# Nine projections of a two-layer block turned from plain fp32 products into three passes over high and low parts

## The chip, the cores and the metric

The kernel runs on one core of a Trainium2 chip. The metric is the device time of one execution in microseconds (us). TensorE multiplies matrices into PSUM (eight banks of 128 x 512 fp32), ScalarE and VectorE work element by element and read PSUM, GpSimd works element by element on SBUF and issues some of the transfers, SyncE issues the stream of weights.

## The reference

Two transformer models of two layers each, one after the other, on 256 tokens of width 1024, all in fp32. Every mixer and every feed-forward is preceded by an RMS norm with a shift and a scale made from a conditioning vector, and followed by a gated residual:

- layer 1: gated linear attention (`gla`), then PEER (`peer_q0`, `u0`, `v0`: product-key routing over 16384 one-neuron experts);
- layer 2: sliding-window attention (`kv`, `swa_q`, `swa_out`), then PEER (`peer_q1`, `u1`, `v1`), then the last norm of the first model;
- layer 3: an mLSTM mixer (`ml_qk`, `ml_v`, `ml_o`, `ml_out`), then a squared-ReLU MLP (`ffn1_0`, `ffn2_0`);
- layer 4: latent attention (`qa` to `ukv_v`, `mla_out`), then an MLP (`ffn1_1`, `ffn2_1`).

A name in brackets is a weight matrix. Those that matter here:

```
gla_out, swa_q, swa_out, ml_v, ml_o, ml_out, mla_out:  y[256,1024] = h[256,1024] @ W[1024,1024]
kv:      y[256,512]  = h[256,1024] @ W[1024,512]
ml_qk:   y[1024,256] = W[1024,1024].T @ h.T   (kept transposed)
```

## The kernel before, in words

All weights stand in one stream in HBM, in slabs of 128 x 2048 fp32 (1 MB), in the order of `PLAN`. SyncE loads them in two halves of 512 KB into `ring`, which has room for two slabs. A half is called a tile (128 x 1024). TensorE is used in two ways:

**Plain.** `gemm_M` and `gemm_T` (lines 580 and 602) multiply the fp32 slab in `ring` as it is. TensorE reads `ring` itself, and SyncE may refill a slab when TensorE has used all of it (`slab_used`).

**In three passes.** The names in `SPLIT` (the PEER and MLP matrices). For each tile ScalarE writes `split_hi` (the tile rounded to fp32r, line 1258), and VectorE or GpSimd writes `split_lo` = tile - `split_hi` (line 1283 on VectorE, in `v0`, `v1` and the second half of `u0`, `u1`; line 1271 on GpSimd, elsewhere). The activations have such parts too. TensorE then adds hi x hi, hi x lo and lo x hi, each product one fp32r matmul. There are two buffers each of `split_hi` and `split_lo`; the semaphores `hi_made`, `lo_made`, `hi_free`, `lo_free` count tiles, and SyncE may refill a half of `ring` when its `split_lo` is made.

The order of work on every engine is written out by hand, and each engine runs its own list in order. Beside the mixers VectorE adds up the conditioning strips ("side chunks", line 426, transfers of 512 KB issued by GpSimd, line 412, into four slots): 16 in the `swa` stage, 40 in `ml`, 24 in `mla`. An out-projection (`*_out`) goes as follows: TensorE turns the mixer's output into PSUM, VectorE copies it to `yT` (line 550), TensorE and VectorE spread the gate over the partitions (lines 453, 464, 472), TensorE multiplies with `last_by_tile=True` (the last products in an order that ends one output bank after the other), VectorE gates and adds the residual bank by bank (lines 692, 703, 705), and the next norm follows. In `peer_q` and `ffn1` the first tile waits for ScalarE's `hi` part of the activations (line 788) and for VectorE's full value and `lo` part (lines 781, 800, `parts_vector`).

```
def used_up(a, tiles, n, e):
    if tiles is None:
        return slab_used, n + (PLAIN[a])
    return lo_made, n * 2 + (tiles + e + 1)
```

Of the kernel before, what the change touches and what calls it, by code (L numbers as in the profile page):

```python
# [34 lines left out]
P = 128  # L35
# [37 lines left out]
SPLIT = ["peer_q0", "u0", "v0", "peer_q1", "u1", "v1", "ffn1_0", "ffn2_0", "ffn1_1", "ffn2_1"]  # L73
# [7 lines left out]
for _name, _n in PLAN:  # L81
    if _name in SPLIT:
# [13 lines left out]
SIDE_STRIPS = {"swa": [10, 11], "ml": [19, 20, 21, 26, 27], "mla": [23, 24, 25]}  # L96
ORDER = (list(range(FIRST_STRIPS)) + V_STRIPS[0] + SIDE_STRIPS["swa"] + V_STRIPS[1] + SIDE_STRIPS["ml"]
         + SIDE_STRIPS["mla"])
# [29 lines left out]
def build(nc, io, marks):  # L128

    new_marks = {}  # L130
    with ExitStack() as ctx:
# [8 lines left out]
        with ExitStack() as scope:  # L140
            scope.enter_context(nc.sbuf_tensor("mlp_room", [P, MLP_ROOM], F32))
            mlp_hi, mlp_lo = (scope.enter_context(nc.sbuf_tensor(n, [P, DC, SEQ], F32R)) for n in ("mlp_hi", "mlp_lo"))
            hid_hi, hid_lo = (scope.enter_context(nc.sbuf_tensor(n, [P, FF // P, SEQ], F32R)) for n in ("hid_hi", "hid_lo"))
        gate = sb("gate", [P, KEYS * SEQ])
# [68 lines left out]
        LAYER = common.at  # L213
        fin_row = yT.rearrange("p a b -> p (a b)")[:, 0:D]
# [415 lines left out]

        def half(nb):
            return slice(nb * BANK, (nb + 1) * BANK)
# [259 lines left out]
        b_flat = b_.rearrange("p a b -> p (a b)")  # L892
        NCH = SEQ // CHUNK

        def gla_tensor(t):
# [71 lines left out]
            gemm_M(t, "gla_out", "gla_out", DC, 2, D, yT, lambda c: [f"gla.on.T{c}"], bank=0, last_by_tile=True)  # L967
# [15 lines left out]
        def gla_scalar(a):  # L983
# [42 lines left out]
            std_scalar(a, "gla.r", 8)  # L1026

        def gla_vector(v):
# [54 lines left out]
            for n in range(NCH - 1):  # L1083
# [18 lines left out]
                .then_inc(vector_steps, v.step())  # L1102
            rstd_vector(v, "gla.r", DV, 8)
# [10 lines left out]
            turned_vector(v, "gla.on", yT, bank=4)  # L1114
            row_store(v, "g1_0", 0)
            v.wait_ge(vector_steps, v.n)
# [36 lines left out]
        def split_gemm_T(t, name, weights, blocks, hi, lo, nbanks=4):  # L1153


            for b in range(blocks):
# [9 lines left out]
                def passes(w, part, src, first=False, last=False):  # L1166
                    for c in range(DC):
                        t.wait_ge(*when(f"{name}.{part}{c}"))
                        ins = nc.tensor.matmul(out, w[:, b % 2, c * P:(c + 1) * P], src[:, c, :],  # L1169
                                               start=(first and c == 0), stop=(last and c == DC - 1))  # L1170
                        if c == 0 and w is split_lo and b or c == DC - 1 and last and not b:
                            ins.then_inc(hi_free, 1)
                    return ins
                passes(split_hi, "hi", hi, first=True)
# [3 lines left out]
                if b:  # L1178
                    passes(split_lo, "hi", hi, last=True).then_inc(lo_free, 1)
                else:  # L1180
                    passes(split_lo, "hi", hi)
                    passes(split_hi, "lo", lo, last=True)
                    nc.tensor.matmul(ps[:, 4, 0:P], zeros[:, :], zeros[:, :], start=True, stop=True).then_inc(lo_free, 1)
# [162 lines left out]
        def peer_choose_vector(v, l):  # L1346
# [5 lines left out]
            parts_vector(v, f"n2_{l}", hT, hT_hi, hT_lo, 4, scale_c, MOD1[l] + SH2, f"pq{l}")  # L1352
# [1312 lines left out]
```

## Time and profile before

| | |
|---|---|
| time, median of 3 runs | 2868.77 us (2868.17 to 2874.35) |
| time of the profiled execution | 2856.19 us |
| its span in the profile | 2854.6 us |
| TensorE busy | 2663.9 us (93% of the span) |
| VectorE, ScalarE, GpSimd busy | 1939.4, 1059.7, 863.3 us |
| mean granted TensorE clock | 0.964 |

The span is what the profiler sees of the program, and the profiled execution's own time is 1.6 us longer. A busy share is one of the whole span; what an edit is worth is read in its own stage. A timeline row gives the start, the duration, the engine, the line, the output and inputs, and in brackets how long the engine had been idle and what released it. TensorE's plain fp32 matmuls have two records each.

### The profile page before, as it was taken

To read this page: it belongs to the slowest core of one execution; us is meant where nothing else is said; L and a number is where in the kernel's file an instruction comes from. 1 tells how busy PE (TensorE), PEld (TensorE's weight loads), DVE (VectorE), ACT (ScalarE), POOL (GpSimd) and SP (SyncE) were. 2 spreads that over 40 slices of the span, in tenths; PEclk is the share of its full clock that TensorE was granted. 3 is DMA by queue.
4 is the path that set the end of the run, shared out by engine and by line. 5 is a ranking of instruction groups with operands and counts; after the bars stand their busy time and mean duration, and the time that the engine had idled before them with its cause. 6 is when DMAs were issued, how large, how long until landed. Compare 5 with 4: busy or idle time off the path is not lost.

```text
span 2854.6 us, 50064 instructions
## 1 busy us (share of the span) xinstructions
PE 2663.9 (93%) x17946; PEld 2258.7 (79%) x17946; DVE 1939.4 (68%) x3229; ACT 1059.7 (37%) x1549; POOL 863.3 (30%) x525
## 2 busy tenths in 40 slices
PE   5988999999999998899999999999988799988898
PEld 4458999999877874679999998778875489755886
DVE  6422997777898774536977778997773579054880
ACT  1214444433434442234444434434441144321443
POOL 2005995000000001047990000000011058810687
PEclk9989999999999998789999999999999899989999
DMA  8524555444467776154555545667876445563454
GB/s 341 214 74 148 170 178 182 160 159 164 167 217 241 273 271 220 36 171 155 177 179 167 161 155 171 207 220 256 274 249 252 175 145 180 193 232 106 148 183 148
DMA packets 147620, 536.83 MB, mean 188 GB/s; under 512 B 16784, under 2 KB 17168, under 8 KB 147232
## 3 DMA queue, kind: packets, MB, share of 16 engines
q1 hardware_dynamic: 115088, 417.08, 43.9%
q0 software_dynamic: 31104, 113.26, 11.4%
q10 hardware_dynamic: 1296, 4.72, 0.4%
q8 instruction: 84, 1.38, 0.2%
q14 instruction: 48, 0.39, 0.0%
HBM read 531.85 MB, written 3.15 MB: 187 GB/s over the span
## 4 chain that ended last, share of the span: by engine, by line
PE 74%; DVE 9%; issue 5%; POOL 4%; DMA 4%; ACT 2%; DVEq 0%; SPq 0%; POOLq 0%; ACTq 0%
PE ps L1596 18%; PE ps L1216 14%; PE ps L602 9%; PE ps L1220 7%; PE ps L2181 5%; POOL split_lo L1271 4%; PE ps L2159 4%; DMA ring<-in_stream 3%; PE ps L1169 3%; PE ps L1554 3%; PE ps L580 2%; PE ps L2163 2%; DVE split_lo L1283 1%; DVE mod_acc L382 1%; PE ps L1753 1%
## 5 line engine op out<-in xcount | busy, mean ns | idle before, releaser
L1258 ACT ACTIVATE split_hi<-ring 128x1024 fp32r<-128x1024 f32 x672 | 708.3, 1055 | 704.3 <-PE ps L1220 447.8
L1271 POOL TENSOR_TENSOR split_lo<-ring,split_hi 128x1024 fp32r<-128x1024 f32 x288 | 745.4, 2601 | 207.1 <-ACT split_hi L1258 206.4
L1283 DVE TENSOR_TENSOR split_lo<-ring,split_hi 128x1024 fp32r<-128x1024 f32 x384 | 468.7, 1221 | 102.4 <-ACT split_hi L1258 102.4
L362 POOL DMA_DIRECT2D mod_w<-in_mod x96 | 50.8, 529 | 1148.2 <-ACT gate L1310 426.5
L1216 PE MATMUL ps<-hT_hi,split_hi 128*128 128x256 f32 x2048 | 292.6, 285 | 4.0 <-ACT split_hi L1258 4.0
L1220 PE MATMUL ps<-hT_hi,split_lo 128*128 128x256 f32 x2048 | 290.0, 284 | 2.4 <-POOL split_lo L1271 2.3
L1216 PE MATMUL ps<-hT_lo,split_hi 128*128 128x256 f32 x2048 | 289.0, 284 | 0.0
L1596 PE MATMUL ps<-split_hi,gate_hi 128*128 128x512 f32 x1024 | 284.9, 399 | 1.1 <-DVE gate_lo L1281 1.1
L1596 PE MATMUL ps<-split_hi,gate_lo 128*128 128x512 f32 x1024 | 276.7, 391 | 2.6 <-DVE gate_lo L1281 2.6
L1596 PE MATMUL ps<-split_lo,gate_hi 128*128 128x512 f32 x1024 | 277.3, 391 | 0.0
L1255 ACT ACTIVATE gate_hi<-gate 128x256 fp32r x256 | 106.9, 418 | 446.0 <-PE ps L1596 446.0
L1220 PEld LDWEIGHTS ps<-hT_hi,split_lo 128*128 128x128 f32 x2048 | 265.4, 193 | 5.2 <-POOL split_lo L1271 5.2
L1216 PEld LDWEIGHTS ps<-hT_hi,split_hi 128*128 128x128 f32 x2048 | 263.1, 191 | 4.4 <-ACT split_hi L1258 4.4
L1216 PEld LDWEIGHTS ps<-hT_lo,split_hi 128*128 128x128 f32 x2048 | 265.5, 193 | 0.0
L1596 PEld LDWEIGHTS ps<-split_hi,gate_lo 128*128 128x128 f32 x1024 | 192.1, 188 | 45.5 <-DVE gate_lo L1281 4.6
L1596 PEld LDWEIGHTS ps<-split_lo,gate_hi 128*128 128x128 f32 x1024 | 191.2, 188 | 44.4 <-DVE split_lo L1283 4.3
L1596 PEld LDWEIGHTS ps<-split_hi,gate_hi 128*128 128x128 f32 x1024 | 187.5, 189 | 38.1 <-ACT split_hi L1258 1.5
L1281 DVE TENSOR_TENSOR gate_lo<-gate,gate_hi 128x256 fp32r<-128x256 f32 x256 | 108.5, 424 | 130.6 <-ACT split_hi L1258 129.6
L602 PE MATMUL ps<-ring,hT 128*128 128x512 f32 (+1 forms) x352 | 156.2, 604 | 12.8 <-DMA ring<-in_stream 9.4
L602 PE MATMUL ps<-ring,gate 128*128 128x512 f32 (+1 forms) x348 | 154.0, 603 | 12.3 <-DMA ring<-in_stream 4.7
L412 POOL DMA_DIRECT2D small<-in_mod x80 | 42.2, 529 | 404.2 <-DVE gate L426 229.0
L692 DVE TENSOR_TENSOR gate<-ps,gate 128x512 f32<-128x512 f32 x32 | 21.9, 688 | 193.6 <-ACT gate L642 157.3
(318 smaller groups left out, 3771.5 us busy)
## 6 DMA issues: line engine op xcount, KB each, us to landing
ring<-in_stream SPq DMA_DIRECT2D x782, 512.0 KB, 4.1
mod_w<-in_mod POOLq DMA_DIRECT2D x96, 512.0 KB, 4.8
small<-in_mod POOLq DMA_DIRECT2D x80, 512.0 KB, 6.2
gate<-in_mod POOLq DMA_DIRECT2D x32, 512.0 KB, 9.4
gate<-in_mod ACTq DMA_DIRECT2D x8, 512.0 KB, 11.6
gate<-in_mod SPq DMA_DIRECT2D x8, 512.0 KB, 10.2
x_kept<-x POOLq DMA_DIRECT2D x4, 512.0 KB, 4.2
gate<-x_kept POOLq DMA_DIRECT2D x4, 512.0 KB, 8.7
```

Of the source, the lines that this page charges most:

```text
L602: return nc.tensor.matmul(ps[:, bank + 2 * nb + i, 0:n], src[:, c, i * P:(i + 1) * P], ring[:, s % RING, at:at + n], start=(c == 0), stop= ...
L1169: ins = nc.tensor.matmul(out, w[:, b % 2, c * P:(c + 1) * P], src[:, c, :], start=(first and c == 0), stop=(last and c == DC - 1))
L1216: nc.tensor.matmul(out, split_hi[:, e, c * P:(c + 1) * P], part[:, c, :], start=(part is hT_hi and c == 0), stop=False)
L1220: ins = nc.tensor.matmul(out, split_lo[:, e, c * P:(c + 1) * P], hT_hi[:, c, :], start=False, stop=(c == DC - 1))
L1255: nc.scalar.activation(gate_hi[:, e, :], at(gate, i, 2 * per * SEQ, (2 * j + e) * SEQ, SEQ), ACT.Copy)
L1258: nc.scalar.activation(split_hi[:, e, :], ring[:, slot, e * D:(e + 1) * D], ACT.Copy).then_inc(hi_made, 1)
L1271: nc.gpsimd.tensor_tensor(split_lo[:, e, :], ring[:, slot, e * D:(e + 1) * D], split_hi[:, e, :].bitcast(F32), ALU.subtract).then_inc(lo_m ...
L1281: nc.vector.tensor_tensor(gate_lo[:, e, :], at(gate, i, 16 * SEQ, (2 * j + e) * SEQ, SEQ), gate_hi[:, e, :].bitcast(F32), ALU.subtract).th ...
L1283: nc.vector.tensor_tensor(split_lo[:, e, :], ring[:, (START[name] + j) % RING, e * D:(e + 1) * D], split_hi[:, e, :].bitcast(F32), ALU.sub ...
L1596: return nc.tensor.matmul(ps[:, 2 * nb + n, :], g[:, e, n * P:(n + 1) * P], w[:, e, nb * BANK:(nb + 1) * BANK], start=False, stop=True, sk ...
L2159: nc.tensor.matmul(out, split_hi[:, e, c * P:(c + 1) * P], part[:, c, :], start=(part is mlp_hi and c == 0), stop=False)
L2181: return nc.tensor.matmul(ps[:, 4 + 2 * nb + n, :], h[:, c0, n * P:(n + 1) * P], w[:, e, nb * BANK:(nb + 1) * BANK], start=(first and h is ...
```

## The change

- `SPLIT` takes in nine more matrices: `gla_out`, `kv`, `swa_q`, `swa_out`, `ml_qk`, `ml_v`, `ml_o`, `ml_out`, `mla_out` (68 tiles). A new `tile_gemm_M` multiplies eight of them, `split_gemm_T` the ninth. ScalarE makes all their `split_hi`, VectorE all their `split_lo`, at places written out between its other work.
- The mixers' outputs and the normed inputs of these get `hi` parts from ScalarE and `lo` parts from VectorE (`turned_hi_scalar`, `turned_lo_vector`, `less_vector`). `less_vector` makes scale x value - hi straight from PSUM and then adds the shift; it takes the place of `parts_vector` in `peer_q` and `ffn1` as well.
- `split_lo` of `peer_q0` and `peer_q1` goes from GpSimd to VectorE, that of the first two tiles of `ffn1_0` and `ffn1_1` too, and that of tiles 4 to 31 of `ffn2_0`.
- Two strips (16 side chunks) go from the `ml` stage to `ffn2_0`; the other side chunks are placed anew among the new subtractions. In `swa_out` four of them, and in `mla_out` three, stand behind the last `split_lo` and ahead of the residual.
- `kv` writes banks 0 and 1 (before 4 and 5), and `swa_q` banks 2, 3, 0, 1, all four waited for at its start.
- In the first tile of `split_gemm_T` and `ffn1` a small matmul on zeros is left out, and the last product of the lo x hi pass ends the tile.

```diff
-SPLIT = ["peer_q0", "u0", "v0", "peer_q1", "u1", "v1", "ffn1_0", "ffn2_0", "ffn1_1", "ffn2_1"]
+SPLIT = ["gla_out", "kv", "swa_q", "swa_out", "ml_qk", "ml_v", "ml_o", "ml_out", "mla_out", "peer_q0", "u0", "v0", "peer_q1", "u1", "v1", "ffn1_0", "ffn2_0", "ffn1_1", "ffn2_1"]
...
-SIDE_STRIPS = {"swa": [10, 11], "ml": [19, 20, 21, 26, 27], "mla": [23, 24, 25]}
+SIDE_STRIPS = {"swa": [10, 11], "ml": [19, 20, 21], "f2_0": [26, 27], "mla": [23, 24, 25]}
...
+        def tile_gemm_M(t, name, weights, slabs, hi, lo, hi_mark, lo_mark, banks, width=D, last_by_tile=False):
+            nbs, per, tiles = width // BANK, D // width, 2 * slabs
+            for nb in range(nbs):
+                for i in range(NT):
+                    for mark in free[banks[2 * nb + i]]:
+                        t.wait_ge(*when(mark))
...
+            for b in range(tiles - (2 if last_by_tile else 0)):
+                for w, src in kinds:
+                    ready(b, w, src)
...
+                    for n in range(per):
+                        for nb in range(nbs):
+                            for i in range(NT):
+                                if b < tiles - 1 or n < per - 1 or src is hi:
+                                    ins = product(b, w, src, n, nb, i)
+                                if w is split_lo and n == nb == i == 0:
+                                    ins.then_inc(hi_free, 1)
...
+        def turned_hi_scalar(a, name, dst, bank=0):
+            for b in range(DC // 2):
+                a.wait_ge(*when(f"{name}.turned{b}"))
+                nc.scalar.activation(dst[:, 2 * b:2 * b + 2, :].rearrange("p a b -> p (a b)"), ps[:, bank + b, :], ACT.Copy) \
+                    .then_inc(scalar_steps, a.step(f"{name}.hi{b}"))
...
+        def less_vector(v, name, tmp, lo, hi, b, bank, sc, sh, mark):
+            v.wait_ge(*when(f"{name}.turned{b}"))
+            v.wait_ge(*when(f"{mark}.hi{2 * b + 1}"))
+            for c in (2 * b, 2 * b + 1):
+                nc.vector.scalar_tensor_tensor(
+                    out=tmp[:, c, :], in0=ps[:, bank + b, (c % 2) * SEQ:(c % 2 + 1) * SEQ], scalar=sc[:, c:c + 1],
+                    in1=hi[:, c, :].bitcast(F32), op0=ALU.mult, op1=ALU.subtract) \
+                    .then_inc(vector_steps, v.step(f"{mark}.less{c}"))
+            for c in (2 * b, 2 * b + 1):
+                v.wait_ge(*when(f"{mark}.less{c}"))
+                nc.vector.tensor_scalar(lo[:, c, :], tmp[:, c, :], modc[:, PLACE[sh], c:c + 1], None, ALU.add) \
+                    .then_inc(vector_steps, v.step(f"{mark}.lo{c}"))
...
-            gemm_M(t, "swa_out", "swa_out", DC, 2, D, yT, lambda c: [f"swa_o.T{c}"], bank=0, last_by_tile=True)
+            out_gemm_tensor(t, "swa_out", "swa_o", swa_y)
...
-            side_chunks_vector(v, "swa", 8, 16)
+            for n in range(7, 16):
+                if n < 13:
+                    less_splits_vector(v, "swa_out", n - 5, n - 4)
+                side_chunks_vector(v, "swa", n, n + 1)
...
-            side_chunks_vector(v, "ml", 31, 40)
+            for n in range(19, 25):
+                less_splits_vector(v, "ml_out", n - 17, n - 16)
+                if n < 24:
+                    side_chunks_vector(v, "ml", n, n + 1)
...
+                           [lambda: side_chunks_vector(v, "mla", 14, 15), lambda: side_chunks_vector(v, "mla", 15, 16),
+                            lambda: less_splits_vector(v, "mla_out", 0, 1), lambda: less_splits_vector(v, "mla_out", 1, 2)])
...
-            side_chunks_vector(v, "mla", 14, 24)
+            for n in range(16, 24):
+                if n < 22:
+                    less_splits_vector(v, "mla_out", n - 14, n - 13)
+                side_chunks_vector(v, "mla", n, n + 1)
...
-                split_lo_gpsimd(g, f"peer_q{l}", 0, 2)
...
-            for name in ("ffn1_0", "ffn2_0", "ffn1_1", "ffn2_1"):
-                if name == "ffn1_1":
+            for l in range(2):
+                if l:
                     side_loads_gpsimd(g, "mla")
-                split_lo_gpsimd(g, name, 0, 4)
+                splits_gpsimd(g, f"ffn1_{l}", 2, 8)
+                split_lo_gpsimd(g, f"ffn1_{l}", 1, 4)
+                if l:
+                    split_lo_gpsimd(g, "ffn2_1", 0, 4)
+                else:
+                    splits_gpsimd(g, "ffn2_0", 0, FFN2_FIRST)
+                    side_loads_gpsimd(g, "f2_0")
```

## Rows read from the trace of the kernel before

**Rows 1.** Timeline of TensorE over the nine projections: start, us, engine, line, count, [idle]

```profile
187.02 27.70 PE L602 MATMUL ps<-ring,gate 128*128 128x512 f32 x64 [0.83 <-DVE gate L472]
...
1100.35 16.83 PE L602 MATMUL ps<-ring,gate 128*128 128x512 f32 x32 [2.22 <-ACT gate L788]
...
1134.33 16.91 PE L602 MATMUL ps<-ring,hT 128*128 128x512 f32 x32 [3.42 <-issue]
...
1222.95 13.97 PE L602 MATMUL ps<-ring,gate 128*128 128x512 f32 x32 [0.38 <-DMA ring<-in_stream]
...
2128.91 2.27 PE L580 MATMUL ps<-hT,ring 128*128 128x256 f32 x7
...
2146.84 15.74 PE L580 MATMUL ps<-hT,ring 128*128 128x256 f32 x64 [3.35 <-DMA ring<-in_stream]
...
2182.62 14.08 PE L602 MATMUL ps<-ring,hT 128*128 128x512 f32 x32 [2.74 <-DMA ring<-in_stream]
...
2218.02 15.67 PE L602 MATMUL ps<-ring,hT 128*128 128x512 f32 x32 [3.33 <-DMA ring<-in_stream]
...
2266.62 27.88 PE L602 MATMUL ps<-ring,gate 128*128 128x512 f32 x64
...
2630.21 13.97 PE L602 MATMUL ps<-ring,gate 128*128 128x512 f32 x32 [1.72 <-DMA ring<-in_stream]
```

**Rows 2.** Timeline in `v0`, then of TensorE in `peer_q0`, both in three passes

```profile
1009.24 0.43 DVE L1281 TENSOR_TENSOR gate_lo<-gate,gate_hi 128x256 fp32r<-128x256 f32 x1
...
1010.15 1.07 PE L1596 MATMUL ps<-split_hi,gate_hi 128*128 128x512 f32 x4
...
1011.06 1.07 PE L1596 MATMUL ps<-split_hi,gate_lo 128*128 128x512 f32 x4
...
254.45 1.12 PE L1169 MATMUL ps<-hT_lo,split_hi 128*128 128x256 f32 x8
255.41 1.12 PE L1169 MATMUL ps<-hT_hi,split_lo 128*128 128x256 f32 x8
```

**Rows 3.** Groups by line: count, then busy us, mean ns of one, idle before it

```profile
L1258 ACT ACTIVATE split_hi<-ring 128x1024 fp32r<-128x1024 f32 x672 | 708.3, 1055 | 704.3 <-PE ps L1220 447.8
L1283 DVE TENSOR_TENSOR split_lo<-ring,split_hi 128x1024 fp32r<-128x1024 f32 x384 | 468.7, 1221 | 102.4 <-ACT split_hi L1258 102.4
...
L426 DVE SCALAR_TENSOR_TENSOR gate<-small,c_act,gate 128x1024 f32<-128x1024 f32 x70 | 89.9, 1285 | 43.1 <-DMA small<-in_mod 38.6
...
L2300 DVE TENSOR_TENSOR hid_lo<-gate,hid_hi 128x512 f32 x32 | 71.2, 2225 | 4.7 <-DVE hid_hi L2298 1.2
```

**Rows 4.** DMA issues between 2200 and 2235 us: KB each, median us to landing

```profile
small<-in_mod POOLq DMA_DIRECT2D x10, 512.0 KB, 7.9
```

**Rows 5.** Timeline, ends of output products and last residual piece behind them: `gla_out`, `v0`, `ml_out`, `ffn2_0`

```profile
215.49 0.69 DVE L703 TENSOR_TENSOR x<-x,gate 128x512 f32<-128x512 f32 x1
...
1089.47 0.39 PE L1596 MATMUL ps<-split_lo,gate_hi 128*128 128x512 f32 x1
...
1091.81 0.69 DVE L703 TENSOR_TENSOR x<-gate 128x512 f32<-128x512 f32 x1
...
2297.60 0.74 DVE L705 SCALAR_TENSOR_TENSOR x<-gate,stat,x 128x512 f32<-128x512 f32 x1
...
2495.64 0.39 PE L2181 MATMUL ps<-split_lo,hid_hi 128*128 128x512 f32 x1
...
2500.20 0.74 DVE L705 SCALAR_TENSOR_TENSOR x<-gate,stat,x 128x512 f32<-128x512 f32 x1
```

**Rows 6.** Timeline, ScalarE's copy of one PSUM bank, and VectorE in the head of `peer_q1`

```profile
1151.28 0.60 ACT L1681 ACTIVATE gate<-ps 128x512 f32<-128x512 f32 x1 [0.26 <-PE ps L602]
...
1251.24 2.64 DVE L800 TENSOR_TENSOR hT_lo<-hT,hT_hi 128x256 fp32r<-128x256 f32 x2
```

**Rows 7.** The chain of waits between `swa_out` and `peer_q1`: start, us, what

```profile
1238.93 7.12 DMA x_kept<-x
```

**Rows 8.** Groups by line on VectorE, 2596 to 2604.6 us (end of the latent attention)

```profile
L1826 DVE TENSOR_TENSOR gate<-ps,gate 128x512 f32<-128x512 f32 x4 | 2.8, 692 | 3.2 <-PE ps L1753 3.2
```

More of the change, by code:

```diff
@@ new lines, in less_splits_vector, with splits_gpsimd @@
+        def less_splits_vector(v, name, first, last):
+            for b in range(first, last):
+                split_lo_vector(v, name, 0, b // 2, b % 2)
+        def splits_gpsimd(g, name, first, last):
+            g.eng.wait_ge(lo_made, TILE0[name] + first)
+            for b in range(first, last):
+                tile = TILE0[name] + b
+                g.eng.wait_ge(hi_made, tile + 1)
+                g.eng.wait_ge(lo_free, tile + 1)
+                nc.gpsimd.tensor_tensor(split_lo[:, b % 2, :], ring[:, (START[name] + b // 2) % RING, (b % 2) * D:(b % 2 + 1) * D],
+                                        split_hi[:, b % 2, :].bitcast(F32), ALU.subtract).then_inc(lo_made, 1)
@@ L1164, in split_gemm_T, with passes @@
                 tile = TILE0[weights] + b
-                def passes(w, part, src, first=False, last=False):
-                    for c in range(DC):
-                        t.wait_ge(*when(f"{name}.{part}{c}"))
+                def passes(w, part, src, chunks=range(DC)):
+                    for c in chunks:
+                        t.wait_ge(*when(f"{source or name}.{part}{c}"))
                         ins = nc.tensor.matmul(out, w[:, b % 2, c * P:(c + 1) * P], src[:, c, :],
-                                               start=(first and c == 0), stop=(last and c == DC - 1))
-                        if c == 0 and w is split_lo and b or c == DC - 1 and last and not b:
+                                               start=(c == 0 and w is split_hi and src is hi),
+                                               stop=(c == DC - 1 and w is split_lo))
+                        if b and c == 0 and w is split_lo:
                             ins.then_inc(hi_free, 1)
                     return ins
-                passes(split_hi, "hi", hi, first=True)
+                passes(split_hi, "hi", hi)
                 if b:
@@ L1178, in split_gemm_T @@
                 if b:
[L1179 removed]
+                    passes(split_lo, "hi", hi).then_inc(lo_free, 1)
                 else:
[L1181 to L1183 removed]
+                    passes(split_lo, "hi", hi, range(DC - 1))
+                    passes(split_hi, "lo", lo).then_inc(hi_free, 1)
+                    passes(split_lo, "hi", hi, range(DC - 1, DC)).then_inc(lo_free, 1)
                 if b % 2:
@@ new lines, in own_less @@
+            def own_less(b):
+                less_vector(v, "n1_1", hT, hT_lo, own_hi, b, 4, scale_c, MOD1[1] + SH1, "n1_1.own")
+            less_splits_vector(v, "kv", 0, 1)
+            kv_less(0)
+            less_splits_vector(v, "kv", 1, 2)
+            kv_less(1)
+            kv_less(2)
+            less_splits_vector(v, "kv", 2, 3)
+            kv_less(3)
+            own_less(0)
+            less_splits_vector(v, "kv", 3, 4)
+            for b in range(3):
+                own_less(b + 1)
+                less_splits_vector(v, "swa_q", b, b + 1)
```

316 lines of the change are left out of this document (242 added, 74 removed).

## The prediction

> **What bounds the kernel now.** I read the engine table first, which names TensorE: 93% busy. What matters is what that time is made of and what stands between the pieces, so I went to TensorE's timeline over the nine projections [rows 1]. Three things are to be seen. A whole projection of 1024 x 1024 takes 27.7 to 27.9 us and half of one 13.97 to 14.08, when TensorE is at full clock. The second slab is waited for at six places, 14.9 us in sum (3.42, 0.38, 3.35, 2.74, 3.33, 1.72): plain products free a slab of `ring` only when all of it is used, so its refill starts late. And after waits of over 3 us (and at `kv`, after a longer one in the norm ahead) a half takes 16.9 or 15.7 instead of 13.9, at the lower of the two clock levels for a while. With start and end halves put together, the nine take about 261 us: `gla_out` 27.7, `kv` 16.8, `swa_q` 34.1, `swa_out` 28.2, `ml_qk` 33.5, `ml_v` 30.8, `ml_o` 32.9, `ml_out` 27.9, `mla_out` 29.8.
>
> **What three passes cost.** The same kernel runs this form elsewhere [rows 2]. In `v0` (512 columns, the shape of `tile_gemm_M`) four products go by every 1011.06 - 1010.15 = 0.91 us, so 2.72 a tile; in `peer_q0` (256 columns) eight every 0.96, so 2.88. I take 2.76 for the eight M projections, near the like row, hence 8 x 2.76 = 22.1 us instead of 27.8, and 11.0 for `kv`. The bounds are 21.8 and 23.0.
>
> Behind that row stands a rule. The Trainium skill, "FP8 and Floating Point Precision", section "TensorE Precision Notes", says that a true fp32 product is made of four passes over high and low parts. By it alone, three passes would be 3/4 of 27.7, or 20.8 us. The rows give 22.1. By the rule the whole would gain 11 us more, about 2803.
>
> **Can the engines feed it?** Each tile needs one `split_hi` of 1.06 us on ScalarE and one `split_lo` of 1.22 on VectorE, and beside 36 of the tiles VectorE also has a side chunk of 1.29 [rows 3]: 1.22 + 1.29 = 2.5 against TensorE's 2.76. That fits, barely. The slab waits go, since half a slab is now free as soon as its `split_lo` is made, and two tiles more stand in the split buffers.
>
> **Part by part**, gain in us of the path that ends the stage:
> - `gla_out`: before, 187.02 to the residual's end at 216.18 [rows 1, 5], 29.2. After: 0.4 for ScalarE's part of the turned output ahead of the first product (a bank copy takes 0.60 [rows 6], overlapped in part), 22.1, and the tail. In a three-pass product that ends by tiles it is 2.64 (`v0`: 1089.86 to 1092.50 [rows 5]; before it was 1.46). 25.1, **+4.0**.
> - `kv` and `swa_q`: before, 1100.35 to 1151.24. `kv` now writes banks 0 and 1 and needn't wait until the turned banks are emptied: start 1.5 earlier, 1098.8 (of the 2.22 idle). It still starts at the lower clock: 16.83 against 13.97, +2.9. Then 11.0. `swa_q` waits at its start for banks 0 and 1, which ScalarE copies out of `kv`: 0.26 + 2 x 0.60 [rows 6] and the drain, 2.2 in all. Then 22.1, and 1.2 as the last bank comes later in the order: 1138.2. **+13.0**, the largest term (bounds 9 to 16).
> - `swa_out`: 29.7 before with its tail, 25.1 after, but four side chunks now stand on VectorE behind the last `split_lo` and ahead of the residual. The last `split_lo` is made about 3 us before TensorE ends; 4 x 1.29 = 5.2 us behind it, with the last subtraction itself, put the residual off by 4.1 at most. **+0.5**. With transfers late (landing 7.9 [rows 4]) it would be a loss of up to 4.
> - `ml_qk`: the first tile is paced by the parts of the input, 16 VectorE instructions of 128 x 256. One subtraction of that size takes 0.43 in `v0` [rows 2]; 0.45 with its start: 7.2, + 0.8 for ScalarE's first part. Then seven tiles at 2.88: 2128.9 + 8.0 + 20.2 = 2157.1, against 2162.6. **+5.5** (bounds 3 to 8).
> - `ml_v`: 30.8 - 22.1 = **+8.7**; `ml_o`: 32.9 - 22.1 = **+10.8**. Slab waits and the low clock behind them are in these.
> - `ml_out`: 31.7 (27.9 + tail of 3.8 [rows 5]) against 0.4 + 22.1 + 4.9 (the tail of `ffn2_0`, the like one by tiles [rows 5]) = 27.4. I take **+4.2**.
> - `mla`: two side chunks and two splits (2 x 1.29 + 2 x 1.22 = 5.0) go into VectorE's waits in the latent attention. These are 3.2 us long [rows 8], and the rest, with one of them in a short gap, is late work: -2.3. `mla_out` itself: 33.6 with its tail, 27.4 after, and 3.5 for three side chunks behind the last split: +2.7. Together **+0.4**.
> - `peer_q0` and `peer_q1`: VectorE's two `lo` parts take 2.64 us beside GpSimd's `split_lo` [rows 6]; two of that size alone take 0.9. GpSimd's share of it goes, and `less_vector` starts from the `hi` part, not behind a full value: 2.0 each. In `peer_q1` the chain also passes over the copy `x_kept` [rows 7], 7.12 us, queued with the weights' transfers; SyncE is ahead of where it was when that copy is issued, so it meets less of them: 2.5 (bounds 0 and 5). `ffn1` heads: 0.9 each, for the same two reasons. Sum **+8.3**.
> - `ffn2_0`: 16 side chunks come in among VectorE's splits. Both fit per tile as above, but the transfers are issued on GpSimd's queue behind its four splits, so the first comes late: **-0.5** (bounds 0 and -2). In `ml` the same 16 go away, which only clears VectorE.
> - The zeros matmul left out, and the stream running up to a slab ahead: nothing, TensorE's 0.1 us at most; the stream is covered by 1 MB per two tiles (5.5 us), the rate at which `v0` already runs with no wait.
>
> On the contention there is a rule too. The Trainium skill, "SBUF — State Buffer", section "Who interferes with whom", says that a VectorE instruction with two SBUF inputs and a GpSimd instruction that reads SBUF hold each other up. The rows agree: L2300 takes 2225 ns for a size that takes 0.69 us elsewhere [rows 3, 5]. It speaks for the heads of `peer_q`. It speaks against the change where VectorE's splits meet GpSimd's (the first tiles of `ffn2_0`); by it these would take some 2 us more.
>
> Sum: 4.0 + 13.0 + 0.5 + 5.5 + 8.7 + 10.8 + 4.2 + 0.4 + 8.3 - 0.5 = 54.9. The profiled execution took 2856.2, which gives 2801.3; it lies 12.6 below the median of the three runs, so I apply the difference to the median: 2868.8 - 54.9 = **2814.0 us**, 1.9% less.
>
> **Rivals.**
> - *VectorE's list stalls on a transfer.* Side chunks stand ahead of splits; if a strip is not there, the split behind it and TensorE wait. For: 38.6 us of idle before L426 are waits for transfers, and one lands 7.9 us after issue [rows 3, 4]. Against: four slots, and strips issued well ahead. If a third of the 80 side chunks cost 1 us, 26 us go: gain 29, **2840**.
> - *The slab waits and the low clock stay.* The stream still delivers 1 MB in its time while TensorE now asks faster. If 14.9 us of waits stay and half of their clock cost, 22 of the 55 are lost: gain 32, **2837**. Against: `v0` and `ffn` run at this rate without waits.
> - *Low clock at the starts.* If six more projections begin as `kv` does, 2.9 us each [rows 1]: +17, **2831**. For: `swa_out`, `mla_out` and `ml_out` follow mixers in which TensorE is often idle. Against: before, those ran in 27.7 to 27.9.
> - *VectorE becomes the bound (slower).* The 36 tiles beside side chunks would go at 1.22 + 1.29 + 7.9/4 = 4.5 us, one transfer latency shared by four slots, not 2.76: 36 x 1.7 = 61, and the tails 5 more: **2880**. It decides from 55/36 = 1.5 us more a tile. Against: in `v0` VectorE makes splits beside its own work at TensorE's pace.
> - *The passes run at 2.88 a tile*, as 256 columns do [rows 2]: 65 x 0.12 = 8 us more, 2822, inside the forecast.
>
> **How the numbers follow.** About 0.2%, 5.7 us, is what a measurement of this kernel tells from no change. The forecast, with its own range of 2803 to 2828 (every bound above taken some way), has 0.65. Stall on side chunks 0.10, slab waits stay 0.09, low clock 0.08, slower 0.04, better than 2803 0.04. The range 2801 to 2840 leaves out the slower case and a few hundredths at each end. Faster 0.94: all but the VectorE-bound case and a sum of several mishaps; within 0.2% 0.02; slower 0.04.
>
> **What would show it.** TensorE four products of 512 columns every 0.91 to 0.96 us in the nine, with no DMA-released idle before the second half. `kv` to `swa_q` a gap of 2.2 us. `swa_out`'s residual starting behind side chunks, some 4 us after TensorE's end, and 3.5 in `mla_out`. VectorE's `split_lo` at 1221 ns still; the two-instruction `lo` of 2.64 us gone from `peer_q1`. Idle before L426 for DMA below 40 us. I would be wrong first in `kv`/`swa_q` (13 us on one order of banks) and in `ml_qk` (0.45 us a piece, read elsewhere); a single long DMA idle on VectorE ahead of a split would show the first rival, and TensorE released by L1283 throughout a projection the VectorE-bound one.

## The result and the profile of the changed kernel

The changed kernel takes 2802.86 us (median of 4 runs, 2793.42 to 2807.53), the kernel before 2868.47. The ratio is 0.9763, 95% interval [0.9733, 0.9793]: 68 us less by the ratio (65.6 by the medians) where 55 were forecast. The ratio times 2868.77, the median that the prediction started from, gives 2800.8 us, just below the range's low end of 2801. Measured again beside other kernels it was 0.9775 [0.9757, 0.9793], about 2804. The sign and most of the mechanism stand, and the gain was taken some 10 us too small; on which side of 2801 the time falls is within the noise of a measurement. The two profiled executions differ by 2856.2 - 2793.4 = 62.8 us.

**The passes.** TensorE's timeline, changed kernel: `kv`, `swa_q`, then `ml_v`, `ml_o`, `ml_out`, `mla_out`.

```profile
1088.26 1.87 PE L657 MATMUL ps<-split_hi,kv_hi 128*128 128x512 f32 x4
...
1103.72 1.17 PE L657 MATMUL ps<-split_hi,own_hi 128*128 128x512 f32 x4 [1.99 <-ACT gate L1818]
...
2123.15 1.32 PE L657 MATMUL ps<-split_hi,ml_hi 128*128 128x512 f32 x4
...
2128.47 1.07 PE L657 MATMUL ps<-split_hi,ml_lo 128*128 128x512 f32 x4
2129.38 1.07 PE L657 MATMUL ps<-split_lo,ml_hi 128*128 128x512 f32 x4
...
2150.48 1.49 PE L657 MATMUL ps<-split_hi,ml_hi 128*128 128x512 f32 x4
...
2206.11 2.70 PE L657 MATMUL ps<-split_hi,ml_y 128*128 128x512 f32 x4
...
2553.51 1.79 PE L657 MATMUL ps<-split_hi,mla_y 128*128 128x512 f32 x4
```

Four products go by every 2129.38 - 2128.47 = 0.91 us, as in `v0` before [rows 2]. From first to last product the projections take: `gla_out` 22.4, `kv` 13.5, `swa_q` 22.5, `swa_out` 23.0, `ml_qk` 27.9, `ml_v` 23.6, `ml_o` 22.4, `ml_out` 24.5, `mla_out` 23.3. Nowhere in them is TensorE released by a load of `ring` any more, as it was in [rows 1]. `swa_q` waits 1.99 us for ScalarE's copies of `kv` (2.2 said). What is above 22.4 stands mostly at the start: the first four products take 1.3 to 2.7 us instead of 1.07. In `ml_out` the granted clock is 0.50 and then 0.69 over its first 4 us, in `ml_v` 0.72 and 0.50, and 1.00 soon after.

**The head of `peer_q0`.** The timeline of the kernel before: the norm's last statistic with GpSimd's subtraction beside it, ScalarE's first parts, VectorE's pair of `lo` parts beside the next subtraction, a wait of TensorE, and the starts of the second and third tile.

```profile
217.22 2.44 DVE L678 SCALAR_TENSOR_TENSOR stat<-stat 128x1 f32<-128x1 f32 x1
217.28 2.35 POOL L1271 TENSOR_TENSOR split_lo<-ring,split_hi 128x1024 fp32r<-128x1024 f32 x1
...
221.96 3.30 ACT L788 ACTIVATE hT_hi<-ps,modc,scale_c 128x256 fp32r<-128x256 f32 x7 [1.11 <-DMA x_kept<-x]
...
227.14 2.63 DVE L800 TENSOR_TENSOR hT_lo<-hT,hT_hi 128x256 fp32r<-128x256 f32 x2
...
231.06 0.72 PE L1169 MATMUL ps<-hT_lo,split_hi 128*128 128x256 f32 x2 [0.86 <-DVE hT_lo L800]
...
231.76 1.62 PE L1169 MATMUL ps<-hT_hi,split_hi 128*128 128x256 f32 x8
...
236.21 1.12 PE L1169 MATMUL ps<-hT_hi,split_hi 128*128 128x256 f32 x8
```

The same in the changed kernel, where the residual ends at 213.09 instead of 216.18:

```profile
212.40 0.69 DVE L844 TENSOR_TENSOR x<-x,gate 128x512 f32<-128x512 f32 x1
...
214.12 0.16 DVE L819 SCALAR_TENSOR_TENSOR stat<-stat 128x1 f32<-128x1 f32 x1
...
216.54 3.75 ACT L929 ACTIVATE hT_hi<-ps,modc,scale_c 128x256 fp32r<-128x256 f32 x8 [1.07 <-DMA x_kept<-x]
...
223.40 1.12 PE L1305 MATMUL ps<-hT_hi,split_hi 128*128 128x256 f32 x8
...
226.28 1.12 PE L1305 MATMUL ps<-hT_hi,split_hi 128*128 128x256 f32 x8
```

A statistic of one column took 2.44 us while GpSimd subtracted, and takes 0.16 now. From the residual's end to the second tile it was 15.6 us and is 10.3. The second tile took 4.45 us and takes 2.88. TensorE waited for nothing within it, before or now; the difference is its clock. The windows of the second tile, before and changed (length, busy PE, PEld, DVE, ACT, POOL, granted clock, DMA share, GB/s):

```profile
231.76:236.21 4.45, 4.45 (x28) 4.45 (x26) 0.00 (x0) 1.87 (x2) 2.43 (x1) 0.62 0.09 38
```

```profile
223.40:226.28 2.88, 2.88 (x27) 2.88 (x26) 1.96 (x2) 1.65 (x2) 0.00 (x0) 1.00 0.31 82
```

Ahead of the slow tile TensorE had waited 0.57 and 0.86 us for `lo` parts. Together that is 6.8 us in this stage.

**The tails.** Timeline of `swa_out`, changed kernel: TensorE's last product, the last of the side chunks behind it, the last residual piece; then `mla_out`, with the copy of the gate row.

```profile
1204.44 0.40 PE L657 MATMUL ps<-split_lo,swa_y 128*128 128x512 f32 x1
1205.23 1.28 DVE L440 SCALAR_TENSOR_TENSOR gate<-small,c_act,gate 128x1024 f32<-128x1024 f32 x1 [0.31 <-DMA small<-in_mod]
...
1211.36 0.69 DVE L844 TENSOR_TENSOR x<-x,gate 128x512 f32<-128x512 f32 x1
...
2576.38 0.40 PE L657 MATMUL ps<-split_lo,mla_y 128*128 128x512 f32 x1
...
2577.57 1.28 DVE L486 COPY gate<-ps 128x512 f32<-128x512 f32 x2
...
2585.26 0.74 DVE L846 SCALAR_TENSOR_TENSOR x<-gate,stat,x 128x512 f32<-128x512 f32 x1
```

VectorE is still at its side chunks when TensorE has ended: 7.2 us from there to the residual's end in `swa_out`, where `gla_out` takes 2.6, and 9.2 in `mla_out`. The chain of waits shows that the last chunk even waited for its transfer:

```profile
1199.64 5.56 DMA small<-in_mod
1205.20 0.03 issue
1205.23 1.30 DVE gate L440
```

**Where the 62.8 us came from**, from the end of one residual to the end of the next (kernel before, changed, gain, forecast). `v1` here includes the last norm of the first model:

| up to | before | changed | gain | forecast |
|---|---|---|---|---|
| `gla_out` | 216.2 | 213.1 | 3.1 | 4.0 |
| `v0` | 876.3 | 869.6 | 6.8 | 2.0 |
| `swa_out` | 145.9 | 129.4 | 16.5 | 13.5 |
| `v1` | 886.1 | 875.6 | 10.5 | 4.5 |
| `ml_out` | 173.9 | 147.8 | 26.0 | 29.2 |
| `ffn2_0` | 202.6 | 201.6 | 1.0 | 0.4 |
| `mla_out` | 147.4 | 149.0 | -1.6 | 0.4 |
| end | 204.5 | 204.0 | 0.5 | 0.9 |

These are one execution against one. The next section says which rows another execution would change.

### The profile page after: what moved, and what is told of

It reads as the page before. It is cut to its first block, busy times and chain, and to the rows that moved or that the text cites. A ratio compares the mean times of both kernels' runs of the same rounds, so it can differ in the third digit from the quotient of the medians.

```text
span 2791.8 us, 50688 instructions
## 1 busy us (share of the span) xinstructions
PE 2608.7 (93%) x18242; PEld 2296.1 (82%) x18242; DVE 2076.6 (74%) x3381; ACT 1145.8 (41%) x1653; POOL 705.2 (25%) x461
## 4 chain that ended last, share of the span: by engine, by line
PE 75%; DVE 10%; issue 5%; POOL 4%; DMA 3%; ACT 3%; DVEq 0%; SPq 0%; POOLq 0%; ACTq 0%
PE ps L1736 19%; PE ps L1353 15%; PE ps L1357 8%; PE ps L657 5%; PE ps L2427 5%; PE ps L1305 4%; POOL split_lo L1408 4%; PE ps L2405 4%; PE ps L616 3%; PE ps L1694 3%; PE ps L2409 2%; DVE split_lo L1420 1%; PE ps L594 1%; DMA ring<-in_stream 1%; DVE mod_acc L396 1%
## 5 line engine op out<-in xcount | busy, mean ns | idle before, releaser
L1395 ACT ACTIVATE split_hi<-ring 128x1024 fp32r<-128x1024 f32 x740 | 779.9, 1056 | 799.9 <-PE ps L1357 447.7
L1420 DVE TENSOR_TENSOR split_lo<-ring,split_hi 128x1024 fp32r<-128x1024 f32 x516 | 629.6, 1221 | 216.2 <-ACT split_hi L1395 215.8
L1408 POOL TENSOR_TENSOR split_lo<-ring,split_hi 128x1024 fp32r<-128x1024 f32 x208 | 546.4, 2643 | 185.3 <-ACT split_hi L1395 184.8
L1613 DVE TENSOR_TENSOR small<-small 128x512 bf16<-128x512 bf16 x384 | 139.5, 419 | 0.0
L1694 PEld LDWEIGHTS ps<-small 128*128 128x128 bf16 x3072 | 96.8, 98 | 36.6 <-DVE small L1613 25.0
L1694 PE MATMUL ps<-small 128*128 128x64 bf16 x3072 | 111.8, 193 | 13.2 <-DVE small L1613 13.2
## 6 DMA issues: line engine op xcount, KB each, us to landing
gate<-in_mod ACTq DMA_DIRECT2D x8, 512.0 KB, 11.5
```

The source lines that it names most:

```text
L1395: nc.scalar.activation(split_hi[:, e, :], ring[:, slot, e * D:(e + 1) * D], ACT.Copy).then_inc(hi_made, 1)
L1408: nc.gpsimd.tensor_tensor(split_lo[:, e, :], ring[:, slot, e * D:(e + 1) * D], split_hi[:, e, :].bitcast(F32), ALU.subtract).then_inc(lo_m ...
L1420: nc.vector.tensor_tensor(split_lo[:, e, :], ring[:, (START[name] + j) % RING, e * D:(e + 1) * D], split_hi[:, e, :].bitcast(F32), ALU.sub ...
L1613: ins = nc.vector.tensor_tensor(pairs(hot_r[r][m]), equal, of_token(2 + m, HALF), ALU.mult)
L1694: ins = nc.tensor.matmul(ps[:, 5 + r % 2, n * HALF:(n + 1) * HALF], hot_c[r % 2][:, n, :], hot_r[r % 2][m][:, n, :], start=(m == 0), stop= ...
```

## What one execution has and another has not

Part of such differences belongs to the execution. In `v1` of the kernel before one strip's transfer came late: VectorE's list stood behind it, and TensorE behind VectorE. The timeline, then the windows:

```profile
1949.22 1.29 DVE L382 SCALAR_TENSOR_TENSOR mod_acc<-mod_w,c_act,mod_acc 128x1024 f32<-128x1024 f32 x1 [1.88 <-DMA mod_w<-in_mod]
...
1950.89 1.21 PE L1596 MATMUL ps<-split_hi,gate_lo 128*128 128x512 f32 x4 [1.60 <-DVE gate_lo L1281]
```

```profile
1948.00:1952.00 4.00, 2.40 (x10) 1.42 (x8) 2.78 (x4) 1.36 (x2) 1.04 (x2) 1.00 0.82 268
1952.00:1956.00 4.00, 4.00 (x12) 3.12 (x12) 3.37 (x5) 1.37 (x2) 0.53 (x1) 0.58 0.90 310
```

A stop of 1.6 us, and then TensorE at a granted clock of 0.58 for some 4 us: `v1` took 402.5 us instead of 399.4. In the changed kernel's repeat the stop is in `v0` (401.2) and `v1` is clean. So the 3.1 us are no part of the change. Likewise `kv` took 13.97 us, not the 16.83 of [rows 1], in a kernel with the same code there (b1 below), and the scores behind `swa_q` took 8.61 instead of 10.76 there. The stage up to `swa_out` took 139.0 us there instead of 145.9, so up to 7 of the 16.5 us in the table are of the execution. The stage up to `mla_out` took 147.4, 153.7 and 146.8 us in three kernels with the old code there (before, b1, b2) and 149.0 to 153.7 in five with the change's, so the table's -1.6 is not clear of this either.

The gla stage ends at 213.1 (twice), 215.1, 220.6, 220.8 and 221.0 us in six executions of code that is the same there. In the late ones the slab wait in `gla_qk` is longer and some 5 us behind it go at the lower clock. The row of the repeat (c0), and its windows:

```profile
61.12 14.16 PE L594 MATMUL ps<-hT,ring 128*128 128x256 f32 x52 [3.83 <-DMA ring<-in_stream]
```

```profile
61.00:66.00 5.00, 4.88 (x12) 3.92 (x13) 2.57 (x2) 0.00 (x0) 1.59 (x3) 0.50 1.03 413
66.00:70.00 4.00, 4.00 (x19) 3.50 (x18) 3.61 (x3) 0.00 (x0) 1.06 (x2) 0.93 1.03 410
```

At the end of `gla_qk` c0 is 4.2 us behind the first execution. The rest of the 7.5 comes later: `gla_v` takes 29.3 us instead of 27.7, again in part at a lower clock, and the slab wait in `gla_og` is 4.2 instead of 3.2.

## The experiments

There are three sets, each on its own chip with its own runs of the kernel before: c0, a1, b1 and a3 (13 runs, median 2869.73), b2, a2, a4 and w1 (11, 2861.9), d1 to d4 (11, 2863.04). A ratio is to the kernel before of its own set; in brackets is its 95% interval.

**c0: the changed kernel again.**

> The changed kernel as it is, once more beside the others: ratio to the kernel before 0.976 to 0.980, some 60 to 68 us less. In its trace v0 and v1 show whether the 3.1 us by which v1 was shorter than before belongs to the change: if it does, v1 takes 399.4 us here too and the kernel before takes 402.5 each time; if it was one late transfer in one execution, either kernel shows such a stall now and then.

2804.29 us, 0.9775 [0.9757, 0.9793]. `v1` 399.4 and a stop in `v0`: one late transfer in one execution, not the change.

**a1: GpSimd makes the weights' remainders in `peer_q0` and `peer_q1` again.**

```diff
-            less_splits_vector(v, f"peer_q{l}", 0, 1)
...
-            less_splits_vector(v, f"peer_q{l}", 1, 2 * PEER_H)
...
+                split_lo_gpsimd(g, f"peer_q{l}", 0, 2)
```

> The changed kernel with the remainders of peer_q0 and peer_q1 made by GpSimd again. Theory: the gain that the prediction lacked came from GpSimd leaving these two stages. Its subtraction of 2.4 us holds up VectorE's small statistics (2.44 us instead of 0.16 in the norm) and one pair of remainders, and paces the second tile (4.4 us instead of 2.9): 5 to 6 us a stage, so 10 to 12 us slower than the changed kernel. Rival: the gain came from less_vector, which makes the remainder without the full value first: then this one is only 2 to 4 us slower.

2810.18 us, 0.9793 [0.9768, 0.9818]: 5.9 us above c0 by the medians, and the intervals overlap. Between theory and rival. By the traces the two `peer_q` end 3.0 and 4.5 us later than in c0.

**b1: the kernel before, with VectorE making these remainders, alone.**

```diff
+            split_lo_vector(v, f"peer_q{l}", 0, 0, 0)
             parts_vector(v, f"n2_{l}", hT, hT_hi, hT_lo, 4, scale_c, MOD1[l] + SH2, f"pq{l}")
+            for b in range(1, 2 * PEER_H):
+                split_lo_vector(v, f"peer_q{l}", 0, b // 2, b % 2)
...
-                split_lo_gpsimd(g, f"peer_q{l}", 0, 2)
```

> The kernel before with this one part of the change alone: VectorE makes the remainders of peer_q0 and peer_q1, with nothing else changed. Theory (GpSimd's contention and pace): 10 to 12 us faster than before, about 0.996. Rival (less_vector): 2 us or less.

2856.43 us, 0.9963 [0.9945, 0.998]: 10.6 us less, the theory's value, with an interval of 5.7 to 15.8 us. The trace shows 3.5 and 4.0 us in the two `peer_q`, 7.5 in all.

**a2: the changed kernel with the old `parts_vector` in these two stages.**

```diff
-            for b in range(DC // 2):
-                less_vector(v, f"n2_{l}", hT, hT_lo, hT_hi, b, 4, scale_c, MOD1[l] + SH2, f"pq{l}")
+            parts_vector(v, f"n2_{l}", hT, hT_hi, hT_lo, 4, scale_c, MOD1[l] + SH2, f"pq{l}")
...
```

> The changed kernel with the old way of making the remainders of the activations in peer_q0 and peer_q1 (full value first, then value minus high part), VectorE keeping the remainders of the weights. Theory after the first runs: moving the weights' remainders gives 3.5 us a stage and less_vector another 3.5: 6 to 7 us slower than the changed kernel. Rival: only GpSimd's leaving counts, under 3 us.

2805.58 us, 0.9795 [0.9769, 0.9822]; the interval covers both. By the traces `less_vector` is worth 0.8 and 0.7 us, so the rival holds. The table has, for `peer_q0` and `peer_q1`, the us from the residual's end to ScalarE's first part, to the second tile and to the last product of `peer_q`, and how long the second tile took at which granted clock. Row b2 is the kernel before with half slabs (below), in which GpSimd still makes the remainders.

| | ScalarE's first part | second tile starts | second tile takes (clock) | `peer_q` ends |
|---|---|---|---|---|
| before | 5.8, 7.7 | 15.6, 17.5 | 4.45 (0.62), 4.44 (0.62) | 60.5, 62.4 |
| b2: earlier loads alone | 5.3, 6.0 | 15.1, 16.2 | 2.96 (1.00), 4.11 (0.68) | 58.6, 60.7 |
| b1: GpSimd gone | 5.3, 7.1 | 13.4, 15.0 | 3.11 (0.95), 2.95 (1.00) | 57.0, 58.4 |
| a1: all but that | 5.3, 6.1 | 13.5, 14.6 | 2.88 (1.00), 4.33 (0.61) | 56.9, 59.4 |
| a2: all but `less_vector` | 3.5, 4.4 | 11.3, 12.3 | 2.88 (1.00), 2.87 (1.00) | 54.7, 55.6 |
| changed (c0) | 3.5, 4.4 | 10.5, 11.5 | 2.88 (1.00), 2.88 (1.00) | 53.9, 54.9 |

The expectation of a1 took the slow second tile for GpSimd's pace. It was the clock: in `peer_q0` of a1, and nearly so in b2, the tile goes at full pace with GpSimd's subtractions beside it, and where it takes 4.1 to 4.5 us the granted clock is 0.61 to 0.68. That happened in four of the six stages with GpSimd, behind waits of TensorE for `lo` parts, and in none of the six without it.

Two things held ScalarE's start, one behind the other. The timeline of b1, then of a1 (`peer_q0`):

```profile
228.62 3.75 ACT L788 ACTIVATE hT_hi<-ps,modc,scale_c 128x256 fp32r<-128x256 f32 x8 [2.87 <-DMA x_kept<-x]
```

```profile
214.14 2.45 DVE L819 SCALAR_TENSOR_TENSOR stat<-stat 128x1 f32<-128x1 f32 x1
...
218.41 3.76 ACT L929 ACTIVATE hT_hi<-ps,modc,scale_c 128x256 fp32r<-128x256 f32 x8 [0.63 <-PE ps L913]
```

With GpSimd gone and the old stream order, the norm is ready but `x_kept` isn't: 2.87 us of waiting. With the changed kernel's stream and GpSimd back, `x_kept` is there (its copies land in 2.9 us, before in 4.1) but the statistic takes 2.45 us. In `peer_q0` GpSimd's leaving alone (b1) gains 0.5 us, the earlier stream without it 0.5 (a1) and 0.4 (b2), and both together 2.3; in `peer_q1` it is 0.6, 1.6 and 1.7, and 3.3. Behind that start and up to the second tile GpSimd's leaving gives 1.6 to 1.9 us more in the kernel before (b1), 1.2 to 1.4 in the changed one (a1), and `less_vector` 0.8. So of the 14.2 us by which the two `peer_q` of c0 end earlier than before, 7.5 go when GpSimd comes back (a1) and 1.5 when `less_vector` goes (a2); the rest is the earlier loads and what these share.

**a3, and d1 again: the side chunks placed elsewhere.**

```diff
+            side_chunks_vector(v, "swa", 7, 8)
             row_store(v, "g1_1", 4)
-            for n in range(7, 16):
-                if n < 13:
-                    less_splits_vector(v, "swa_out", n - 5, n - 4)
+            side_chunks_vector(v, "swa", 8, 10)
+            for n in range(10, 16):
+                less_splits_vector(v, "swa_out", n - 8, n - 7)
                 side_chunks_vector(v, "swa", n, n + 1)
...
-                           [lambda: side_chunks_vector(v, "mla", 14, 15), lambda: side_chunks_vector(v, "mla", 15, 16),
-                            lambda: less_splits_vector(v, "mla_out", 0, 1), lambda: less_splits_vector(v, "mla_out", 1, 2)])
+                           [lambda: side_chunks_vector(v, "mla", 14, 15)] + 3 * [lambda: None])
...
-            for n in range(16, 24):
-                if n < 22:
-                    less_splits_vector(v, "mla_out", n - 14, n - 13)
+            less_splits_vector(v, "mla_out", 0, 2)
+            side_chunks_vector(v, "mla", 15, 18)
+            row_store(v, "mla_out.g", 4)
+            for n in range(18, 24):
+                less_splits_vector(v, "mla_out", n - 16, n - 15)
                 side_chunks_vector(v, "mla", n, n + 1)
-            post_rest_vector(v, "mla_out", 4, 0, "m2_1")
+            v.wait_ge(vector_steps, v.n)
+            tile_post_vector(v, "mla_out", "m2_1", 0)
```

> The changed kernel with the side chunks of swa_out and mla_out placed elsewhere: three of swa_out ahead of its third split, one behind the last; in the latent attention one chunk instead of two chunks and two splits, then both splits, three chunks and the copy of the gate row in VectorE's idle 7 us before the third split. Theory: VectorE's tail costs 4.6 us in swa_out and 5.1 in mla_out, and the four pieces in the attention 2.6: 9 to 12 us faster than the changed kernel. Rival: the tail only hides a wait for the side chunks' transfers or for TensorE, which comes back: under 4 us.

> The version with the side chunks moved, measured again beside the next three, because its ratio and theirs came from calls in which the kernel before itself read 2869.7 and 2861.9. Expected 0.970 to 0.973.

a3: 2786.85 us, 0.9712 [0.9692, 0.9733], 17 us below c0, which ran beside it, and the intervals are apart. d1: 2789.33, 0.9755 [0.9723, 0.9786], above the 0.970 to 0.973 expected; against c0's ratio, of another set, that is 6 us. How much it is worth as a time stays between these. The traces agree with each other: the tail is 2.85 us instead of 7.2 in `swa_out`, 5.1 instead of 8.9 to 9.7 in `mla_out`, and the stage up to `mla_out` takes 141.4 and 141.2 us against 149.0 to 153.7. The end of `swa_out` in a3:

```profile
1215.56 0.39 PE L657 MATMUL ps<-split_lo,swa_y 128*128 128x512 f32 x1
...
1218.11 0.69 DVE L844 TENSOR_TENSOR x<-x,gate 128x512 f32<-128x512 f32 x1
```

So the change's placing of these twelve pieces cost some 12 us by the trace. The rival (a transfer that comes back as a wait) falls: VectorE's idle time for these transfers is 6.3 and 6.1 us, in c0 9.6.

**b2: the kernel before, all plain, slabs released and awaited by halves** in every plain projection but those of the latent attention.

```diff
-                    return slab_used, n + (PLAIN[a])
+                    return half_used if e == 0 and a != START["qa"] else slab_used, n + (PLAIN[a])
...
+                if weights in HALVED and c % per == per // 2 - 1:
+                    ins.then_inc(half_used, 1)
...
```

> The kernel before, all products plain as before; alone, a half of a slab may be refilled as soon as TensorE has passed it, and TensorE waits for a slab's halves one by one, in all plain projections but those of the latent attention. It tells how much of the change's gain is the end of the slab waits, and how much the three passes. Theory (the prediction's split): 13 us of waits in these stages and about 7 of low clock behind them go, and some 4 in the gla stage: 20 to 28 us faster than before; the three passes carry the other 40. Rival: the loads, not the release, are late, and TensorE waits as long for halves: under 8 us.

2828.38 us, 0.9875 [0.9849, 0.9901]: 36 us less by the ratio, 33.5 by the medians, more than the 20 to 28 expected, with no product changed. `gla_qk` now runs through. This is its timeline, and then `ml_qk`:

```profile
49.79 21.32 PE L592 MATMUL ps<-hT,ring 128*128 128x256 f32 x98
...
2105.75 19.60 PE L592 MATMUL ps<-hT,ring 128*128 128x256 f32 x86
2124.76 9.66 PE L592 MATMUL ps<-hT,ring 128*128 128x256 f32 x44
```

The stage up to `gla_out` takes 207.1 us (before: 216.2, in b1 223.4), up to `swa_out` 136.2 (145.9, 139.0), up to `ml_out` 163.0 (173.9, 173.8). So of the change's 26 us in `ml` 10.9 are the end of the slab waits with the clock behind them, and 15.2 are the rest of the change, the passes above all.

**d2, a4 and d3: half slabs in what stays plain in the gla stage** (`gla_qk`, `gla_v`, `gla_og`), alone and with the side chunks moved. The edit is that of b2, with

```diff
+        HALVED = ("gla_qk", "gla_v", "gla_og")
```

> The version with the side chunks moved, and besides the three plain projections that are left in the gla stage release and await their slabs by halves. Theory: the waits of 1.2 to 3.8 us in gla_qk and the low clock behind them, which make that stage 213 us in one execution and 221 in another, go: 5 to 9 us faster than with the side chunks moved alone, the stage at 212 us or less each time. Rival: its transfers are late because VectorE's strips load at the same time, and nothing changes.

> The changed kernel with half slabs in the gla stage alone, side chunks where the change put them. Theory: the stage goes from 213 or 221 us to 203 in every execution: 10 to 17 us faster than the changed kernel, 0.971 to 0.974. Rival (the earlier ratios, 0.9712 without and 0.9706 with halves): no measurable gain, 0.976 to 0.978, the transfers saved here being waited for elsewhere.

> Side chunks moved and half slabs in the gla stage. Theory: the two gains add, 9 to 17 us below the side chunks moved alone, 0.966 to 0.969. Rival: equal to it within 3 us.

d2: 2792.82 us, 0.9751 [0.9723, 0.9779], between theory and rival. a4: 2777.57, 0.9706 [0.968, 0.9733], 9 us below a3 by the medians but only 2 by the ratios, which are of two sets. d3: 2780.74, 0.9716 [0.9687, 0.9746], 8.6 us below d1 of the same set, just short of the 9 expected, and the two intervals overlap. The times alone don't settle it. By the traces the stage up to `gla_out` takes 203.1 to 203.3 us in these three, 202.8 and 206.9 in w1 and d4 below, which have the same code there, and 213.1 to 221.0 in the six executions without halves. No slab wait is left in any of the five. In d4 the granted clock over `gla_qk` is lower (0.89 from 41 to 80 us, 0.94 to 1.00 in the others). So the theory's waits and some 10 us hold, but not that the stage takes 203 us every time.

**w1, and d4 again: products of zeros in TensorE's idle stretches.**

```diff
+            keep_busy(t, 6, 20)
             turned_out_tensor(t, "ml_turn", ml_h, lambda i, c: f"ml.gated{i}")
+            keep_busy(t, 6, 6)
...
```

`keep_busy(t, bank, count)` multiplies 128 x 128 zeros `count` times into a free bank. There are 26 such products ahead of `ml_out`, and 6 each ahead of `swa_out` and `mla_out`.

> The same with TensorE kept busy by products of zeros in its idle stretches ahead of swa_out, ml_out and mla_out (6, 26 and 6 of them). Theory: ml_out takes 24.3 us instead of 22.4 because it starts at the lower clock (2 us), mla_out and swa_out 0.9 and 0.6 more than 22.4: 2 to 4 us faster. Rival: the clock doesn't rise for so few products, or they delay the next real one: no gain, or 1 to 2 us slower.

> The same with the products of zeros. The trace of the first run showed the gate row's four products at 1.98 us instead of 3.42 to 3.78 and ml_out at 23.0 instead of 24.3: 2 to 5 us below the one without them. Rival: within 1 us, as the first ratio said.

2777.35 us, 0.9699 [0.9672, 0.9726], and 2779.66, 0.9706 [0.9678, 0.9734]: 0.2 and 1.1 us below the same kernel without them (a4, d3), less than the 2 to 5 expected and nothing that can be told apart. `ml_out` does take 23.0 us instead of 24.3 and 24.4, and the gate row's four products ahead of `swa_out` take less. The timeline of w1, then of a4:

```profile
1165.96 1.50 PE L1987 MATMUL ps<-zeros 128*128 128x128 f32 x12
...
1169.27 1.98 PE L478 MATMUL ps<-gate,ones 128*128 128x512 f32 x4 [1.80 <-DVE gate L467]
```

```profile
1173.80 3.42 PE L478 MATMUL ps<-gate,ones 128*128 128x512 f32 x4 [3.14 <-DVE gate L467]
```

That is 2 to 3 us a kernel, within what one late transfer gives or takes.

## Why the prediction was right or wrong

- **What three passes cost**: right. 22.4 us at full clock (22.1 said), 0.91 us per four products. The Trainium skill, "FP8 and Floating Point Precision", section "TensorE Precision Notes", gives four passes for a true fp32 product; by it alone three would take 20.8 us. A plain product takes 27.7/32 = 0.87 us, 0.217 a pass, and a pass that stands alone takes 0.227 to 0.233. So the traces fit the rule's count, and the 20.8 was too low because a pass of its own is 5 to 8% dearer.
- **The heads of `peer_q`, +8.3 with `ffn1`**: this is the step that failed, a term mis-sized. "2.0 each" measured 6.8 and 7.6 us (up to the last product of `peer_q`), and `ffn1` 1.8 and 1.1 instead of 0.9 each. So 17.3 us where 8.3 were said, and 9 us is what the sum lacked. I priced the one contended pair of rows that I showed, 2.64 us [rows 6], and put at nothing two things beside it: GpSimd's hold on the norm's statistic (2.44 us instead of 0.16), and the lower clock in the second tile behind TensorE's waits (4.45 us at a granted 0.62 instead of 2.88 at 1.00). I gave the wait for `x_kept` 0.5 us, in `peer_q1` alone [rows 7], where it is part of ScalarE's later start in both stages (2.3 and 3.3 us), and I did not see that it and the statistic cover each other. The Trainium skill, "SBUF — State Buffer", section "Who interferes with whom", names the pair VectorE with two SBUF inputs and GpSimd. The traces agree, and show it for operands of one column too.
- **`kv` and `swa_q`, +13.0**: 58.7 us became 43.6, +15.1. Order and wait came as said, the start 2.2 us earlier (1.5 said), `kv` took 13.5 (13.9 said) and `swa_q` 22.5 (23.3 said). But the term owes part of its size to the one execution that I read: in b1, with the old code, the same stretch takes 53.4 us, `kv` 13.97 of it instead of 16.83, and against that the gain is 9.9.
- **`swa_out`, +0.5**: -0.5. The delay behind four side chunks was 4.6 us (4.1 said), one wait for a transfer in it.
- **`ml_qk`** +5.8 (+5.5 said), **`ml_o`** +10.5 (+10.8). **`ml_v`** +7.2 (+8.7) and **`ml_out`** +2.4 (+4.2): both start at the lower clock (0.50 to 0.72 over their first 4 us), the third rival in small, 3.3 us together where it was given 17.
- **`gla_out`**: +4.1 on its own (+4.0), but 1.0 us was lost ahead of it in this pair. Two `split_lo` stand there in front of the mixer's last statistics; that they cost it is not shown, since the stretch from `gla_og` to `gla_out` takes 34.5 and 35.4 us with the old code (b1, before) and 34.9 to 36.3 with the new.
- **`mla`, +0.4**: -1.6. In this pair the pieces in the attention cost 2.6 (2.3 said), and `mla_out` with its tail gained 1.5 (2.7 said). The tail was 9.2 us: three side chunks, and behind them the copy of the gate row (1.28), which I left out.
- **Slab waits go**: right in the nine, and b2 shows their price. Rival two fell. What stays plain keeps its waits, 1.0 to 4.0 us each in the changed kernel's gla and latent attention stages. Rival one (VectorE's list stalls) fell too: its idle time for side chunks' transfers went down, 38.6 us [rows 3] to 7.1 (9.6 in c0). Rival four (VectorE the bound) fell: behind the first tile of each of the nine, TensorE has no idle of more than 0.3 us that VectorE ended. Rival five rested on a count of 65 tiles; beside `ml_qk` there are 60, which makes its 8 us 7.
- **The range**: its low end stood 13 us under the forecast and gave 0.04 to what lay below. The bounds of the one term that I had read from the page least closely, the heads, were written down for `x_kept` alone. A range that took 0 to 10 us on them would have held. As it was, the time fell 0.2 us outside, and noise had a part in that.
- Still open: why, in one execution and not in another, the slab wait in `gla_qk` is 1.3 or 3.8 us long. No run tells. Nor does a run take the new order of banks in `kv` and `swa_q` alone, so how their gain divides is argued from the rows. And what decides whether the clock falls behind the waits in the first tile of `peer_q` is not shown.

## What to carry to other kernels

When work leaves an engine that shares SBUF with another, price every instruction of the other that stood beside it, statistics of one column included, and look at TensorE's granted clock behind each wait, not just at the widest row. Where two things hold one start, taking away either alone shows little (0.5 us of 2.3 here), so try both. Before products are made cheaper, look at how late their buffers are freed: releasing `ring` by halves gave the kernel before 36 us, about half of what the whole change gives, in a few lines. Much of that is the same gain, since the change frees halves too; in the gla stage, which the change leaves plain, halves give some 10 us more. The best version run here (half slabs, side chunks moved) takes 2777.6 and 2780.7 us, 0.971 and 0.972 of the time before.

## What the runs showed of the hardware

- A stop of TensorE of 1.6 us can be followed by some 4 us at a granted clock near one half (0.58 over 4 us): `v1` took 3.1 us more with it than without. Two waits of 0.57 and 0.86 us in the first tile of `peer_q0` were followed by 4.45 us at 0.62; in b2 waits of the same length were not (1.00), so such a wait does not decide it alone.
- A VectorE instruction with two operands of a single column took 0.16 us alone and 1.81 to 2.48 us while GpSimd subtracted 128 x 1024 (2.4 us). In all six cases (before, a1, b2) it ended within 0.03 us of GpSimd's, whether it had started 0.06 us before it or 0.6 us after.
- Single executions of the kernel before range from 2851.4 to 2877.7 us; its profiled one, 2856.2, is among the fastest. A difference of a few us in one stage of one pair of profiles needs a second pair.
